# Output projection of a decoder trunk's mixer in seven half-size products per pair of token tiles, with record places found by the eight largest

## The reference

```python
x = x + merge_branches(gates, y_mla, y_conv, y_mem, w_out)     # (tokens x 1024) @ (1024 x 1024)
h = rms_norm(x, g_ffn_norm)
scores = sigmoid(h @ w_router)                                 # 64 experts
_, top_idx = top_k(scores + b_router, 8)
top_w = scores[top_idx] / sum(scores[top_idx]) * 2.5
x = x + routed_experts(h, top_idx, top_w) + swiglu(h, w_s_gate, w_s_up, w_s_down)
```

## Time and profile before

| | before |
|---|---|
| median of 3 runs | 2406.03 us (2401.39 to 2409.67) |
| the profiled execution's own time | 2402.07 us |
| its span | 2400.3 us |
| TensorE busy in the span | 2341.0 us (98%) |
| VectorE, ScalarE, GpSimd busy | 1141.2, 561.6, 863.8 us |
| granted TensorE clock, mean over the span | 0.993 of full speed |
| stage_mixer, first to last matmul | 1353.65 to 1557.5 us |

### The profile page before, as it was taken

The page is one execution under the profiler, slowest core; times in us unless marked ns, Lnnn a source line. Parts: engine busy times, 40 slices in busy tenths (PEclk is TensorE's granted clock), DMA queues, the critical chain, the costliest instruction groups (busy, mean ns, idle before and its releaser), DMA issues. The chain is left out here.

```text
span 2400.3 us, 36797 instructions
## 1 busy us (share of the span) xinstructions
PE 2341.0 (98%) x12668; PEld 1714.4 (71%) x12668; DVE 1141.2 (48%) x2476; ACT 561.6 (23%) x1284; POOL 863.8 (36%) x639
## 2 busy tenths in 40 slices
PE   8999999999999999999999999999999999999997
PEld 5886666666668888766656666668777777877775
DVE  5431555555746666459895355443323233333231
ACT  2001344343523333310013111101111111111111
POOL 1000000000004665600000035457676666776774
PEclk9999999999999999999999999999999999999999
DMA  7521032322238566263113521089999999999995
GB/s 236 171 78 55 27 92 81 94 69 82 69 77 202 153 145 168 80 189 83 40 54 101 161 87 45 10 336 328 319 341 320 345 346 345 354 353 355 338 347 145
DMA packets 288267, 433.32 MB, mean 181 GB/s; under 512 B 125194, under 2 KB 217790, under 8 KB 269626
## 3 DMA queue, kind: packets, MB, share of 16 engines
q1 hardware_dynamic: 250322, 351.45, 44.3%
q0 software_dynamic: 30016, 67.79, 11.3%
q10 hardware_dynamic: 7744, 11.72, 1.4%
HBM read 375.84 MB, written 87.46 MB: 193 GB/s over the span
## 5 line engine op out<-in xcount | busy, mean ns | idle before, releaser
L2948 PEld LDWEIGHTS pGe<-xT,we_g 128*128 128x128 f32 x2048 | 261.8, 191 | 33.5 <-issue 33.5
L2948 PE MATMUL pUe<-xT,we_u 128*128 128x128 f32 (+4 forms) x2048 | 269.7, 289 | 2.6 <-issue 2.4
L2948 PE MATMUL pGe<-xT,we_g 128*128 128x128 f32 (+4 forms) x2048 | 270.8, 290 | 0.2 <-DVE xT L2846 0.2
L2948 PEld LDWEIGHTS pUe<-xT,we_u 128*128 128x128 f32 x2048 | 261.5, 191 | 4.3 <-issue 4.0
L2725 POOL DMA_INDIRECT mergedT<-tokens_normed,gather_rows x204 | 209.4, 1026 | 77.6 <-issue 63.1
L1661 PE MATMUL pKs<-ws_uk_q,cTs 128*128 128x260 f32 x1024 | 233.5, 384 | 0.0
L2958 PE MATMUL pYe<-we_d,first_w 128*128 128x512 f32 x512 | 230.2, 592 | 0.8 <-DVE first_w L2852 0.8
L1337 POOL TENSOR_TENSOR rk<-ssk,half 128x32 f32<-128x32 f32 x32 | 172.9, 5428 | 133.6 <-DVE ssk L1493 133.6
L1661 PEld LDWEIGHTS pKs<-ws_uk_q,cTs 128*128 128x128 f32 x1024 | 190.6, 190 | 32.8 <-issue 4.3
L2852 DVE TENSOR_TENSOR first_w<-mergedT,pUe 128x256 f32<-128x256 f32 (+4 forms) x64 | 29.3, 459 | 341.0 <-PE pUe L2948 280.9
L2784 ACT ACTIVATE mergedT<-pYe,wc 128x512 f32<-128x512 f32 x128 | 87.8, 687 | 383.5 <-PE pYe L2958 363.0
(11 more groups left out here) (490 smaller groups left out, 3797.0 us busy)
## 6 DMA issues: line engine op xcount, KB each, us to landing
we_g<-in_w_e_gate SPq DMA_DIRECT2D x64, 1024.0 KB
we_u<-in_w_e_up SPq DMA_DIRECT2D x64, 1024.0 KB
we_d<-in_w_e_down SPq DMA_DIRECT2D x64, 1024.0 KB
latents_in_order<-in_cache_latent SPq DMA_DIRECT2D x128, 128.0 KB
lat_quarters<-latents_in_order SPq DMA_DIRECT2D x256, 64.0 KB, 2.1
mergedT<-latents_in_order SPq DMA_DIRECT2D x8, 2048.0 KB, 12.2
first_w<-in_w_in SPq DMA_DIRECT2D x10, 512.0 KB, 5.0
raw_columns<-raw_out SPq DMA_DIRECT2D x32, 129.0 KB, 2.1
```

Of the source, the lines that this page charges most:

```text
L2948: mm = pe.matmul(dst[p][:, f * CAP:f * CAP + n], w[r][:, k, f * P:(f + 1) * P], xT[p][:, k, 0:n], start=k == 0, stop=k == KD - 1)
```

## The change

1. Tiles 3 to 8 are projected in three pairs (3,4), (5,6), (7,8). The two tiles' 256 rows by 1024 of the contraction, times 1024 by 1024, is taken as a 2 x 2 by 2 x 2 product of blocks and computed with seven block products (Winograd's form of Strassen's) in place of eight. A block product is 128 rows by 512 of the contraction by 512 columns. DVE makes four sums of `w_out`'s blocks once (`weight_sum`; three in new tiles, one in place) and four sums of the tiles' blocks per pair (`row_sum`). Eleven adds of 512 columns per pair make the outputs from the products (`first_sums`, `middle_sums`, `later_sums`, `last_sum`); ScalarE copies the first product to SBUF (`take_first`).
2. x is loaded straight into `keep.x2`, where the sums are made: tiles 1 and 2 by one DMA ahead of the router's weights and the constants, tiles 3 to 8 by one DMA behind them. The per-tile x loads of the loop are gone.
3. `prefix` is gone. A token's eight places are the eight largest values of (place + 1) x mask, found by one `max` instruction.
4. All orders are written anew, except GpSimd's, which is as it was. In the first pair DVE runs `average(2)` and `normalise(2)` alone ahead of `place(0)`; in the pairs with t = 5 and t = 7, it runs `average(t-2)`, `average(t-1)`, `normalise(t-2)`, `normalise(t-1)`, `place(t-3)`, `first_sums`, `choose(t-2)`, ...

The diff, cut to its core:

```diff
+    PLAIN = 3
+    PAIRS = (NTT - PLAIN) // 2
+    PRODUCTS = (1, 2, 6, 5, 7, 3, 4)
...
+                sp.dma_start(keep.x2_s[0:DB, :], a["x_sample"].rearrange("b s d -> (b s) d")).then_inc(x_in[0], 16)
+                x_load(0, PLAIN - 1, 1)
                 sp.dma_start(w_r[:, :, :], a["w_router"][0].rearrange("(k p) n -> p k n", p=P)).then_inc(S["router_in"], 16)
...
-                x_load(1)
+                x_load(PLAIN - 1, NT, 2)
...
-                    sp.wait_ge(S["x2_ready"], t + 1)
-                    if t + 2 < NTT:
-                        x_load(t + 2)
...
+                def take_first(pair):
+                    act.wait_ge(S["prod"], 7 * pair + 1)
+                    if pair:
+                        act.wait_ge(S["prod_used"], 4 * pair - 2)
+                    act.activation(m1[:, :], bank_of(7 * pair), ACT.Copy).then_inc(S["m1_ready"], 1)
...
-                v.wait_ge(S["small_in"], 128)
+                v.wait_ge(S["small_in"], 112)
...
+                def row_sum(pair, i):
+                    first, second = {1: (left_of(pair, 2, 1), left_of(pair, 2, 2)), 2: (sum_of(1), left_of(pair, 1, 1)),
+                                     3: (left_of(pair, 1, 1), left_of(pair, 2, 1)), 4: (left_of(pair, 1, 2), sum_of(2))}[i]
+                    if pair:
+                        v.wait_ge(S["prod"], 7 * pair - 7 + {1: 4, 2: 4, 3: 5, 4: 6}[i])
...
+                    v.tensor_tensor(sum_of(i), first, second, ALU.add if i == 1 else ALU.subtract).then_inc(S["row_sums"], 1)
...
+                def first_sums(pair):
+                    t = PLAIN + 2 * pair
+                    if pair == 0:
+                        v.wait_ge(x_in[2], 16)
+                    v.wait_ge(S["m1_ready"], pair + 1)
+                    marks.mark(v.tensor_tensor(x_half(t, 0), x_half(t, 0), m1[:, :], ALU.add))
+                    marks.wait(v)
+                    take(pair, 2, x_half(t, 0), x_half(t, 0)).then_inc(S["prod_used"], 1)
+                    take(pair, 6, u2[:, :], m1[:, :]).then_inc(S["prod_used"], 1)
...
-                    marks.mark(v.tensor_tensor(picked[0:r, :, :], sel[0:r, :, :], spread(dest[0:r, :], TOPK), ALU.mult))
+                    marks.mark(v.scalar_tensor_tensor(posm[0:r, :], dest[0:r, :], 1.0, mask[0:r, :], ALU.add, ALU.mult))
                     marks.wait(v)
-                    marks.mark(v.tensor_reduce(dest8[0:r, :], picked[0:r, :, :], AX.X, ALU.add))
+                    marks.mark(v.max(out=dest8[0:r, :], in_=posm[0:r, :]))
                     marks.wait(v)
+                    marks.mark(v.tensor_tensor(sel[0:r, :, :], spread(posm[0:r, :], TOPK), spread(dest8[0:r, :], NE, 2), ALU.is_equal))
...
+                for i in range(1, 5):
+                    row_sum(0, i)
+                weight_sum(1)
+                weight_sum(2)
+                add(0)
+                average(0)
+                weight_sum(4)
+                normalise(0)
...
+                for pair in range(PAIRS):
+                    t = PLAIN + 2 * pair
+                    if pair:
+                        average(t - 2)
+                    average(t - 1)
+                    if pair:
+                        normalise(t - 2)
+                    normalise(t - 1)
+                    place(t - 3)
+                    first_sums(pair)
+                    choose(t - 2)
+                    middle_sums(pair)
...
+                    place(t - 2)
+                    later_sums(pair)
...
+                    choose(t - 1)
+                    last_sum(pair, 3)
...
+                    last_sum(pair, 4)
+                average(NT - 1)
+                average(NT)
+                normalise(NT - 1)
+                normalise(NT)
+                place(NT - 2)
+                choose(NT - 1)
...
+                for pair in range(PAIRS):
+                    t = PLAIN + 2 * pair
+                    product(pair, 1)
+                    rank(t - 3)
+                    product(pair, 2)
+                    turn(t - 2)
+                    product(pair, 6)
+                    route(t - 2)
+                    product(pair, 5)
+                    turn(t - 1)
+                    rank(t - 2)
+                    product(pair, 7)
+                    route(t - 1)
+                    product(pair, 3)
+                    product(pair, 4)
+                rank(NT - 2)
+                shared(0, (0,))
+                turn(NT - 1)
+                shared(0, (1,))
                 route(NT - 1)
                 turn(NT)
```

More of the change, by code:

```diff
@@ L2178, in stage_mixer @@
         ebase = c.sb("expert_base", [P, NE])
-        kth = c.sb("kth", [P, TOPK])
-        pre = [c.sb(f"prefix{i}", [P, GR + NE]) for i in range(2)]
         posm = c.sb("chosen_place", [P, NE])
@@ L2198, in stage_mixer @@
         PARTS = ((P, 384), (384, 640), (640, D))
-        x_in = [c.sem(f"f_x_in{p}") for p in range(2)]
+        x_in = [c.sem(f"f_x_in{p}") for p in range(3)]
         h2_stored = [c.sem(f"f_h2_stored{p}") for p in range(2)]
@@ L2212, in x2_of, with bank_of, left_of, sum_of @@
             return keep.x2[:, t - 1, :] if t else keep.x2_s[0:DB, :]
+        def bank_of(n):
+            return pX[n // 2 % 2][:, n % 2 * ND:(n % 2 + 1) * ND]
+        def left_of(pair, row, k_half):
+            return keep.mergedT[:, (k_half - 1) * HK:k_half * HK, cols_of(PLAIN + 2 * pair + row - 1)]
+        def sum_of(i):
+            return row_sums[:, i - 1, :, :]
         def unit_of(j):
@@ new lines, in x_half, with take @@
+                def x_half(t, half):
+                    return x2_of(t)[:, half * ND:(half + 1) * ND]
+                def take(pair, i, out, other):
+                    n = 7 * pair + PRODUCTS.index(i)
+                    v.wait_ge(S["prod"], n + 1)
+                    return v.tensor_tensor(out, bank_of(n), other, ALU.add)
+                def first_sums(pair):
[7 more added lines that the diff above has]
+                    take(pair, 6, u2[:, :], m1[:, :]).then_inc(S["prod_used"], 1)
@@ L2348, in average, with last_sum @@
+                def last_sum(pair, i):
+                    t = PLAIN + 2 * pair + (i == 4)
+                    half = x_half(t, int(i == 3))
+                    take(pair, i, half, half).then_inc(S["x2_ready"], 1)
                 def average(t):
@@ L2476, in _ @@
                 unit(1)
-                prefix(NT)
                 place(NT)
@@ L2518, in project_samples, with product @@
                     mm.then_inc(S["x2_psum"], 1)
+                def product(pair, i):
+                    at = PRODUCTS.index(i)
+                    n = 7 * pair + at
+                    if at == 4:
+                        pe.wait_ge(S["m1_ready"], pair + 1)
+                    elif at > 4:
+                        pe.wait_ge(S["prod_used"], 4 * pair + at - 4)
+                    elif pair == 0:
+                        pe.wait_ge(S["x2_ready"], PLAIN)
+                    elif at < 2:
+                        pe.wait_ge(S["prod_used"], 4 * pair - 1 + at)
+                    else:
+                        pe.wait_ge(S["x2_ready"], PLAIN + 2 * pair - 3 + at)
+                    if i in (5, 6, 7, 3):
+                        pe.wait_ge(S["row_sums"], 4 * pair + {5: 2, 6: 2, 7: 3, 3: 4}[i])
+                    if i in (4, 5, 6, 7):
+                        pe.wait_ge(S["w_sums"], {5: 2, 6: 2, 4: 3, 7: 4}[i])
+                    lo, hi = slice(0, HK), slice(HK, KD)
+                    left = {1: left_of(pair, 1, 1), 2: left_of(pair, 1, 2), 3: sum_of(4), 4: left_of(pair, 2, 2), 5: sum_of(1), 6: sum_of(2), 7: sum_of(3)}[i]
+                    if i < 3:
+                        rows = lo if i == 1 else hi
+                        right = [(0, P, keep.first_w[:, rows, :]), (P, ND, w_out[:, rows, 0:ND - P])]
+                    else:
+                        right = [(0, ND, {3: w_out[:, hi, B12], 4: t4[:, :, :], 5: t1[:, :, :], 6: t2[:, :, :], 7: w_out[:, lo, B12]}[i])]
+                    for at, end, w in right:
+                        for k in range(HK):
+                            mm = pe.matmul(bank_of(n)[:, at:end], left[:, k, :], w[:, k, :], start=k == 0, stop=k == HK - 1)
+                    mm.then_inc(S["prod"], 1)
                 def turn(t):
                     r = rows_of(t)
+                    if t >= PLAIN:
+                        pe.wait_ge(S["prod"], 7 * ((t - PLAIN) // 2 + 1))
                     pe.wait_ge(S["h2_ready"], t + 1)
@@ L2567, in _ @@
                 project(1, ((640, D),))
[L2568 to L2582 removed]
+                project(2, ((0, P), (P, 512)))
+                turn(0)
+                project(2, ((512, D),))
+                route(0)
+                for pair in range(PAIRS):
+                    t = PLAIN + 2 * pair
+                    product(pair, 1)
[15 more added lines that the diff above has]
+                shared(0, (1,))
                 route(NT - 1)
```

170 lines of the change are left out of this document (95 added, 75 removed).

## The result

| | before | after |
|---|---|---|
| median | 2407.72 us of 4 runs (2401.39 to 2409.67) | 2424.43 us of 4 runs (2421.47 to 2426.51) |
| profiled execution, its span | 2402.07, 2400.3 us | 2424.79, 2423.0 us |
| granted TensorE clock, mean | 0.993 | 0.988 |
| first matmul of `stage_mixer` to first matmul of the experts' stage | 1353.65 to 1560.33 = 206.68 us | 1353.71 to 1580.03 = 226.32 us |

The change makes the kernel slower: the ratio is 1.0078 [1.0064, 1.0091], the forecast was 2423.1 us. Of the 22.7 us between the two spans, 19.6 arise in the stage. I count them as scatter between executions.

A forecast was written before the change was run, and what follows sets the result against it. TensorE was taken to bound the stage. -10.7 + 5.8 + 5.7 + 7.4 + 3.8 + 5.1 = +17.1 us, added to the median 2406.03, gave 2423.1 us; own range 2415 to 2429, eight in ten 2409 to 2431.

The forecast's parts named there:

- `turn(6)` and `rank(5)`: Third pair, behind record(3): TensorE waits 1.0 us at turn(6) and 6.4 at rank(5), 7.4 together.
- Columns: TensorE in the three pairs: seven block products in place of eight save 3.56 us per pair, 10.7 for three.
- Start: VectorE starts at 1373.3 after late constants, with row and weight sums ahead of add(0): TensorE waits 5.8 us at project(2).
- Joins: Where pairs meet, a power behind GpSimd's record delays TensorE: 5.7 us at rank(3), 7.4 at the third pair, 3.8 at turn(8).
- T + 22.7: Time of the mask of choose(3) on VectorE, T being the start of average(3); rank(3) then waits 5.7 us.
- Records: GpSimd's record taken as long beside a VectorE normalisation; if it starts first, 0.8 us shorter, 2.4 over three joins.
- Clock: TensorE loses clock behind four gaps, 1.7 us each, 6.8; 1.7 of it is given back, leaving 5.1 us.
- worst rival: The same as (C), where each gap costs 2.6 us of clock: 2431.6 us; chance 0.13 together with (D).
- (A): GpSimd's powers come in time, so the joins' waits go: 2402.8 us, no change, or 2398.1, faster; chance 0.11.
- (B): Waits are there but small: early start and no clock loss 2415.0 us, with shorter records and landing 2410; chance 0.14.
- (C): Waits and clock both dear: landing of 3.38 us, +5, each gap at 2.6, +3.5: 2431.6 us; chance 0.13 with (D).
- (D): TensorE's products exceed 3.46 us: 21 groups lose a fill of 0.15 us each, +3; inside (C), chance 0.13 together.

The follow-up runs named there:

- fourth experiment: Against the changed kernel, GpSimd's powers ahead of the records, x load behind the constants and first sums behind add(0): 2389.76 us, ratio 0.9946 to before.
- fifth: Against the changed kernel, only the x load of tiles 1 and 2 moved behind the constants, sums left in place: 2410.55 us, timed once.
- sixth experiment: Against the changed kernel, only VectorE's first sums moved behind add(0), x load left ahead of the constants: 2405.06 us, timed once.
- first experiment: Against the changed kernel, only GpSimd's list changed, both powers of a pair ahead of both records: 2398.23 us, ratio 0.9994 to before.
- second experiment: Against the changed kernel, only VectorE's order changed in the second and third pair, normalise(t-1) behind choose(t-2): 2406.45 us, ratio 1.0026 to before.
- last experiment: Against the changed kernel, matmuls with unread results put on TensorE ahead of rank(3), rank(5) and turn(8): 2408.67 us, ratio 1.0050 to before.
- first four experiments: The first experiment, second experiment, fourth experiment, and one changing the start alone (x load behind constants, sums behind add(0)) against the changed kernel: 2412.18 us.

## Why the prediction was right, step by step

The forecast was 2423.1 us and 2424.43 was measured. The sum was +17.1 us of stage; the trace shows +19.6, in these terms:

| term | predicted | measured | from |
|---|---|---|---|
| seven products | -10.7 | -10.6 | fourth experiment, 3 x 3.53 |
| gap at `project(2)` | +5.8 | +5.95 | row of the gap |
| `rank(3)` | +5.7 | +4.5 | could start 1450.74, started 1455.20 |
| `turn(6)` and `rank(5)` | +7.4 | +4.4 | 1488.55 to 1492.97 |
| `turn(8)` | +3.8 | +3.3 | 1520.72 to 1524.01 |
| clock | +5.1 | +10.0 | below |
| `route(2)`, once | 0 | +1.2 | row of the gap |
| first product, landing of `w_out` | 0 | +0.4, +0.3 | waits |
| `rank(0)`, a wait of before that is gone | 0 | -0.3 | waits |

That is 19.1 of 19.64. The forecast met the measured median to 1.3 us, and missed the stage by 2.5.

*Columns.* Right to 0.1 us, by one pair of the fourth experiment.

*Start.* Right in size, and for the reason given, though the constants landed at 1374.2, later than the 1373.3 I had taken and than my upper bound of 1373.5. The timeline of VectorE:

```profile
1374.18 0.69 DVE L2403 TENSOR_TENSOR row_sums<-mergedT 128x512 f32<-128x512 f32 x1 [20.79 <-DMA expert_base<-in_k_ebase]
...
1381.31 1.77 DVE L2374 TENSOR_TENSOR x_sample<-pXf,x_sample 8x128 f32<-8x128 f32 x5
```

The fifth and sixth experiments part its two causes: the load put back takes 2.5 us off the gap, the sums put back take it away whole, and the late landing then costs nothing. The landing was mis-sized in two parts: the load delays VectorE's start by 2.3 us and not 3.1, and without the load VectorE starts 18.2 us behind the stage's first matmul, as it does before (1371.83), where the 1370.3 I had built on is 16.7 behind.

*Joins.* The mechanism, its three places and its order (`rank(3)`, `rank(5)`, `turn(8)`) are as predicted, and the first two experiments show it from both ends. The sizes are too high. By its own steps the prediction's T + 22.7 should be T + 22.6. From the end of `power(3)` to the start of `power(4)` pass 11.73 us, where I had 12.65: the first DMA of the record took 1.07 and not 1.84, and the landing 1.33 and not 1.65 (the 1.65 of the earlier trace rows ended with VectorE's mean, so it was only an upper bound). The DMA started 0.5 us ahead of the normalisation, the case that the prediction names under *Records* as worth 0.8 us. `place(2)` took 4.06 and the sums 1.92, a little less than I had. At the third pair I had let the last sums come later than they did: `average(5)` starts 0.81 us behind the pair, as `average(3)` does; there is no wait at `turn(6)`, and the second join is as long as the first. In total 12.2 in place of 16.9. VectorE's idle time ahead of the normalisation, 10.36 us, was predicted as 11.5.

*Clock.* Here the step failed in size: the price of a gap, 1.7 us, was taken too low for three of four. I had taken 1.7 for each gap and 1.7 given back, from one row of 1.64 behind a gap of 2.84. Measured are, over the full-clock durations: at the start 3.26 less 1.84, so 1.4; at the first join 0.5 in `rank(3)` and 2.5 in the product behind it (6.16 less 3.65), 3.0; at the second 0.5 and 2.4, 2.9; at the end 0.9 in `turn(8)` and 1.8 in the half unit (6.61 less 4.79), 2.7. My upper bound of 2.6 per gap, written for the worst rival, is exceeded by these three. That some of it is given back, because TensorE is late, is true at one place: 1.4 us at the second join. In the pair slowed by the first join, VectorE waits for TensorE ahead of its last sum:

```profile
1470.96 0.69 DVE L2411 TENSOR_TENSOR x<-pXf,x 128x512 f32<-128x512 f32 x1 [1.50 <-PE pXf L2659]
```

In the last experiment, where the first join has full clock, VectorE does not wait there, `average(5)` starts 2.2 us behind the pair in place of 0.81, and `rank(5)` starts 6.66 us behind `turn(6)` in place of 5.29. So the 4.4 us of the table at `rank(5)` are less by this 1.4, and part of the prediction's 7.4 was right for a pair at full clock. The start's loss is not given back at all: the first join waits 4.26 us in the sixth experiment, which has no start gap, and 4.29 here. The clock of the stretches behind each gap:

```profile
1383.00:1387.00 4.00, 3.86 (x18) 3.65 (x19) 2.49 (x4) 1.15 (x2) 2.48 (x1) 0.62 1.10 353
1455.00:1459.00 4.00, 3.80 (x8) 2.25 (x9) 3.72 (x10) 0.00 (x0) 2.99 (x3) 0.50 0.02 1
1459.00:1463.00 4.00, 4.00 (x14) 2.06 (x14) 3.73 (x15) 0.00 (x0) 3.18 (x3) 0.73 0.02 1
...
1524.00:1528.00 4.00, 3.99 (x12) 3.09 (x13) 3.72 (x15) 2.00 (x2) 0.00 (x0) 0.50 0.32 131
```

The rule of the Trainium skill ("TensorE: Matmul & The Clock Gate", section "HAM oscillation — how this bites in real kernels") that a kernel pays for every long wait again agrees with the stretches right behind the four gaps (0.62, 0.50, again 0.50 from 1493 to 1497, and 0.50); it does not with the fifth experiment, whose clock is 1.00 from 1381 to 1385, behind a gap of 3.43.

How much a gap costs did not follow from its length here. Behind 5.91 us in the first experiment and 5.95 here it is 2.6 and 1.4 (9.70 and 8.52 us for `project(2)`'s first groups, less the 7.14 at full clock in the fifth), behind 3.13 in the second experiment and 3.12 here 1.5 and 2.7. So one row was a poor price, and a row behind a gap of the like length would have been one too. The two errors, 4.7 too much for the joins and 4.9 too little for the clock, nearly cancel: the forecast's closeness is partly luck.

*`route(2)`.* I had predicted no wait in the first pair. TensorE waits 1.18 us there: `route(2)` starts at 1424.22, when ScalarE's `take_h(2)` is done (1424.12), and that started only at 1423.10, 3.9 us behind the end of `turn(2)`. VectorE resumes with `place(1)` at the same time, 1423.16, behind a wait of 1.34 us that the page calls "remote". The first four experiments show this wait of VectorE (1.20 to 1.23 us) and none shows the one of TensorE; the others show neither. Its cause stays open.

*Rivals.* (A), the powers in time, is false for the change as it stands, but the first experiment is (A) made true, and it gives what (A) said: a stage 1.3 us shorter than before, 2398.23 against 2401.13, no difference that can be measured; (A) had -3.2. (B) is false: start and clock are both there. (C) has half: the clock is dearer than it says (10.0 us against 8.6), the landing is not. (D) is false, products stand 3.44 to 3.49 us apart. The experts' stage does start untouched.

## What to carry to other kernels

When requests are brought together (two norms side by side in place of one per tile), look at the list of the engine that serves them, above all when the change does not touch it: one small instruction behind eight DMAs and their landing is 12 us late on an engine whose busy share is a third. Then look at what stands behind the waiting instruction on its own engine, and let only what needs it stand there; here either remedy takes most of the loss at the joins away. Where TensorE bounds and waits, count the wait and the slow clock behind it as two costs; here three waits of 12.2 us took 8.6 more. Over all the experiments such a wait, of 3.1 to 4.3 us, took 1.5 to 3.0 more, so give the second cost a wide range.

## What the runs showed that I had not expected

- A GpSimd instruction of 0.55 us before, the first power, took 2.61 us beside `weight_sum(4)` on VectorE, which reads two SBUF inputs for 2.3 us (1384.37 to 1386.71):

```profile
1384.52 2.61 POOL L2272 TENSOR_TENSOR r_f<-n_f,minus_half 8x1 f32<-8x1 f32 x1 [29.85 <-DVE n_f L2449]
```

It ended 0.4 us behind the sum. The first DMA of a record took 1.07 us beside a normalisation here and 2.08 in the first experiment. What differs is which starts first. Here the DMA starts 0.49 us ahead of the normalisation (1434.76 and 1435.25), and it is the record's second DMA, begun inside it, that is long, 1.24. In the first experiment the DMA starts 0.15 us behind (1435.57 and 1435.42), before the change 0.37 us behind, and takes 2.08 and 1.84. All three of the long ones end 0.8 to 1.0 us behind the normalisation. No run varies this order alone.

- An issue of a DMA took SyncE longer with more ahead of it: the norm's weights took 3.86 us to issue before and 4.05 in the fifth experiment, and 6.97 here and 6.83 in the sixth, with 1.05 MB more in the queue. The constants behind it are issued 2.9 us later than before:

```profile
1360.24 6.97 SPq L2249 DMA_DIRECT2D g_ffn<-in_g_ffn_norm  x1
...
1369.62 0.43 SPq L2249 DMA_DIRECT2D expert_base<-in_k_ebase  x1
```

- What a gap costs in clock does not grow with it in these runs: none behind 1.12, 1.52 and, at the stage's start, 3.43 us; 1.4 behind 5.95; 3.0 behind 4.29; 1.5 (5.13 less 3.65) in the product behind 5.56; 1.7 (5.35 less 3.65) behind 1.74, and the same 1.7 behind the first rank's 4.26 of the fifth experiment:

```profile
1451.39 5.35 PE L2659 MATMUL pXf<-w_out,row_sums 128*128 128x512 f32 x8
```

What decides between these is not settled.
